# Sixty-eight sums of GpSimd move to VectorE and ScalarE, with 20 pause lists and 9 places of modulation chunks

## What is computed

```python
# first block
merged = sigmoid(gate_a) * y_a + sigmoid(gate_b) * y_b
x = x + merged @ w_out
h = rms_norm(x, ln2)
x = x + (silu(u_gate) * u_val) @ w_down          # u = causal_dwconv(h @ w_up)
# second block, for each of two layers
mod = silu(c) @ w_mod + b_mod                    # shift, scale, gate
h = rmsnorm(x, norm_gain) * (1 + scale) + shift
dots = einsum('bqhd,bsd->bqhs', q_idx, k_idx)    # indexer: 16 heads of 64
I = einsum('bqh,bqhs->bqs', w_idx, relu(dots))
sel = top_k(where(causal, I, -inf), 64)
logits = q_a @ k_a * scale + bias[rel]           # only where selected
att = softmax(logits) @ v_a
x1, x2 = halves(q_b or k_b)                      # rotary
rotated = [x1 * cos - x2 * sin, x1 * sin + x2 * cos]
ret = retention(q_b, k_b, v_b)                   # two chunks of 128
x = x + gate * (concat(att * silu(g_a), groupnorm(ret) * silu(g_b)) @ w_out)
```

## Time and profile before

| | us |
|---|---|
| median of 3 runs | 1931.37 (1929.94 to 1937.82) |
| the profiled execution, its own time | 1930.03 |
| its span on the core | 1928.2 |
| PE busy | 1834.6 (95%) |
| DVE busy | 1688.6 (88%) |
| ACT busy | 1230.3 (64%) |
| POOL busy | 213.0 (11%) |
| DMA engines, share of the span | 81.3% |
| granted TensorE clock, mean share | 0.979 |

### The profile page before, as it was taken

How to read it: one execution, slowest core, us unless ns; L and a number is a source line. 1 busy time by engine, 2 the same in 40 slices (tenths; PEclk the granted TensorE clock), 3 DMA queues, 4 the chain that set the end, 5 groups by cost and what they waited for, 6 DMA issues and landing times.

```text
span 1928.2 us, 33543 instructions
## 1 busy us (share of the span) xinstructions
PE 1834.6 (95%) x13102; PEld 1715.3 (89%) x13102; DVE 1688.6 (88%) x2199; ACT 1230.3 (64%) x1907; POOL 213.0 (11%) x140
## 2 busy tenths in 40 slices
PE   6999999999999999999999999899999999998998
PEld 5888899999997899889998997889889888987897
DVE  7897997988798799999999897898898889898896
ACT  6667654744664675656766667756668775657773
POOL 0000031031010001122000000042110003132000
PEclk9998999999999999999999999999999999999999
DMA  8887876968898897788999997877888878786985
GB/s 291 266 273 242 281 240 219 311 198 289 298 356 320 282 313 237 258 289 295 308 321 348 329 331 242 285 248 253 266 278 308 276 231 296 233 277 222 325 297 183
DMA packets 258523, 535.81 MB, mean 278 GB/s; under 512 B 23609, under 2 KB 28734, under 8 KB 257342
## 3 DMA queue, kind: packets, MB, share of 16 engines
q1 hardware_dynamic: 257933, 531.44, 81.3%
q10 hardware_dynamic: 432, 2.23, 0.3%
HBM read 531.50 MB, written 2.10 MB: 277 GB/s over the span
## 4 chain that ended last, share of the span: by engine, by line
PE 46%; DVE 10%; issue 4%; ACT 4%; DMA 1%; POOL 1%; SPq 0%; ACTq 0%; DVEq 0%
PE ps L151 46%; DVE ring_r L1900 3%; ACT w L1456 1%; DVE AR_r L1900 1%; DMA ring<-in_w_in 1%; POOL AR L2498 1%; DVE macc L1900 1%; ACT stg L1462 1%; DVE stg L1897 1%; DVE stg L1892 0%; ACT AR L1456 0%; DVE stg L1900 0%; ACT AR L1462 0%; DVE AR L1892 0%; DVE AR L2369 0%
## 5 line engine op out<-in xcount | busy, mean ns | idle before, releaser
L1900 DVE SCALAR_TENSOR_TENSOR ring_r<-ring,w 128x1024 fp32r<-128x1024 f32 x495 | 616.2, 1265 | 94.4 <-ACT w L1456 93.8
L1456 ACT ACTIVATE w<-ring 128x1024 fp32r<-128x1024 f32 x495 | 510.9, 1055 | 173.0 <-PE ps L151 84.6
L151 PE MATMUL ps<-hh_r,w 128*128 128x256 f32 (+1 forms) x3500 | 505.3, 287 | 7.1 <-ACT w L1456 5.6
L151 PEld LDWEIGHTS ps<-hh_r,w 128*128 128x128 f32 (+1 forms) x3500 | 453.1, 191 | 14.7 <-issue 7.0
L151 PE MATMUL ps<-hlo,ring_r 128*128 128x256 f32 x3108 | 435.9, 283 | 1.5 <-DVE ring_r L1900 1.5
L151 PEld LDWEIGHTS ps<-hlo,ring_r 128*128 128x128 f32 x3108 | 399.8, 190 | 1.7 <-DVE ring_r L1900 1.7
L1900 DVE SCALAR_TENSOR_TENSOR AR_r<-AR,w 128x1024 fp32r<-128x1024 f32 (+1 forms) x150 | 187.3, 1260 | 30.6 <-ACT w L1456 30.6
L151 PE MATMUL ps<-AR 128*128 128x64 f32 (+5 forms) x1316 | 181.8, 296 | 18.5 <-DVE AR L1896 6.2
L151 PEld LDWEIGHTS ps<-AR 128*128 128x128 f32 (+1 forms) x1316 | 165.2, 196 | 28.1 <-issue 9.9
L1456 ACT ACTIVATE w<-AR 128x1024 fp32r<-128x1024 f32 (+1 forms) x150 | 154.4, 1045 | 52.4 <-PE ps L151 31.2
L1900 DVE SCALAR_TENSOR_TENSOR macc<-ring,sm,macc 128x1024 f32<-128x1024 f32 x131 | 177.1, 1352 | 0.1
(11 more groups left out here) (221 smaller groups left out, 2269.4 us busy)
## 6 DMA issues: line engine op xcount, KB each, us to landing
ring<-in_w_in SPq DMA_DIRECT2D x313, 512.0 KB, 5.0
ring<-in_w_mod SPq DMA_DIRECT2D x142, 512.0 KB, 5.4
ring<-in_w_up SPq DMA_DIRECT2D x126, 512.0 KB, 5.3
ring<-in_w_down SPq DMA_DIRECT2D x66, 512.0 KB, 5.7
AR<-in_w_in SPq DMA_DIRECT2D x64, 512.0 KB, 5.5
ring<-in_w_out SPq DMA_DIRECT2D x64, 512.0 KB, 5.8
AR<-in_w_up SPq DMA_DIRECT2D x50, 512.0 KB, 5.5
AR<-in_w_mod SPq DMA_DIRECT2D x37, 512.0 KB, 5.6
```

Source lines behind the costliest of these rows:

```text
L151: return e.matmul(o, l, x, start=start, stop=stop, skip_group_check=True)
L1456: return e.activation(o, i, ACT.Copy, scale=scale)
L1900: return e.scalar_tensor_tensor(o, a, s, b, op0, op1)
```

## The change

The 68 sums of the four kinds leave POOL. Those of `merge`, `sparse` and `rot` (40) become `tensor_tensor` instructions on DVE in the same segment. In the indexer, segments 1 to 7, ACT takes the relu from the banks (4 activations a segment, 56 in all, on the same two pieces of each bank), and DVE multiplies by the weight and adds to the running sum in one `scalar_tensor_tensor` that reads the staging buffer and the sum, both in SBUF (4 a segment, in place of 4 `tensor_scalar`). The banks now go back when ACT is through, the staging buffers when DVE is.

In the tables, 20 pause lists are new or changed, for `bias`, `convk` (k, 2), `convq` (q, 3), `gdn` (2), `indexer` (1), three `modend`, four `retain`, two `sparse` and six `xpose`; and `MODS` gains nine entries. Most segments that move do so by one to four chunks; segments 13 to 21 of `bias` stand three chunks later and 22 to 37 seven.

```diff
-    ('bias',): (2, 2, 4, 1, 2, 4, 6, 0, 4, 1, 2, 4, 1, 2, 4, 1, 2, 4, 1, 2, 4, 1, 2, 4, 1, 2, 4, 1, 2, 4, 1, 2, 4, 1, 2, 4, 1),
+    ('bias',): (2, 2, 4, 1, 2, 4, 6, 0, 4, 1, 2, 4, 4, 2, 4, 1, 2, 4, 1, 2, 4, 5, 2, 4, 1, 2, 4, 1, 2, 4, 1, 2, 4, 1, 2, 4, 1),
...
-    ('retain', 1, 3): (4, 5, 2, 3, 4, 1, 1), ('setup',): (2, 2, 0, 1, 1), ('sparse', 0, 1): (4, 1, 1, 4, 3, 1),
...
+    ('sparse', 0, 1): (2, 3, 1, 4, 3, 1), ('sparse', 0, 3): (5, 1, 0, 5, 3, 1), ('xpose', 1, 0): (3, 1, 1),
...
@@ USES
-                *[f"+a +b +s +z -s@idx_pool.g0{i} -z@idx_pool.g1{i} -a@idx_dve.a{i} -b@idx_dve.b{i}"
+                *[f"+a +b +s +z -s@idx_dve.b{i} -z@idx_dve.b{i} -a@idx_act.a{i} -b@idx_act.b{i}"
...
@@ scalar_program
+        def indexer(J, seg):
+            L, = J.at
+            if 1 <= seg < 8:
+                hold(e, J, "s", "z")
+                x0, x1 = pair(st(J, "s")[:, 0:256]), pair(st(J, "z"))
+                e.wait_ge(*idx_pe.after(f"p{seg}", L))
+                for hf, bk in ((0, pb(J, "a")), (1, pb(J, "b"))):
+                    fn(x0[:, hf, :], bk[:, 0:128], ACT.Relu)
+                    fn(x1[:, hf, :], bk[:, 128:384], ACT.Relu).then_inc(*idx_act.step(f"{'ab'[hf]}{seg}", L))
...
-                e.wait_ge(*merge_pool.after("sum", blk, hf))
+                e.wait_ge(*merge_dve.after("sum", blk, hf))
@@ vector_program, merge
+                k = 4 * blk + 2 * hf
+                e.wait_ge(*merge_dve.after("gate", blk, hf))
+                e.wait_ge(*yb_dve.after(f"y{hf}", blk))
+                tt(s_, s_, flat2(GBT[:, k:k + 2, :]), ADD).then_inc(*merge_dve.step("sum", blk, hf))
@@ vector_program, indexer
+                        e.wait_ge(*idx_act.after(f"{'ab'[hf]}{seg}", L))
+                        e.wait_ge(*idx_dve.after(f"{'ab'[hf]}{seg - 1}", L))
+                        stt(a0[:, hf, :], x0[:, hf, :], wi[:, 0, hd:hd + 1], a0[:, hf, :], MUL, ADD)
+                        stt(a1[:, hf, :], x1[:, hf, :], wi[:, 1, hd:hd + 1], a1[:, hf, :], MUL, ADD).then_inc(*idx_dve.step(f"{'ab'[hf]}{seg}", L))
@@ vector_program, sparse
+                e.wait_ge(*idx_dve.after("sel1", L))
+                e.wait_ge(*bias_act.after("e11"))
+                if hp > 0:
+                    e.wait_ge(*sp_pe.after("pv", L, hp - 1))
+                tt(L0, B0[:, h0:h0 + 2, :], mid(MN0, 2), ADD).then_inc(*sp_dve.step("l0", L, hp))
+                tt(L1, B1[:, h0:h0 + 2, :], mid(MN1, 2), ADD).then_inc(*sp_dve.step("l1", L, hp))
                 e.wait_ge(*sp_pe.after("qk", L, hp))
                 e.wait_ge(*qn_dve.after("inv", L, hp))
-                e.wait_ge(*sp_pool.after("l1", L, hp))
+                e.wait_ge(*sp_dve.after("l1", L, hp))
@@ vector_program, rot
+                e.wait_ge(*rot_dve.after("m", *J.at))
+                tt(d, d, zv, ADD).then_inc(*rot_dve.step("sum", *J.at))
@@ pool_program: merge, indexer, sparse and rot are gone
```

More of the change, by code:

```diff
@@ L219 @@
                "+f -f@sp_act.out"],
-    "rot": ["+z", "-z@rot_pool.sum"],
+    "rot": ["+z", "-z@rot_dve.sum"],
     "retain": ["+s +z +a +b -a@ret_dve.s0 -b@ret_dve.s1", "+c -c@ret_act.out", "", "", "",
@@ L390, in program @@
     gb_act, yb_dve = signal("gb_act"), signal("yb_dve")
-    merge_act, merge_dve, merge_pool = (signal(f"merge_{n}") for n in ("act", "dve", "pool"))
+    merge_act, merge_dve = (signal(f"merge_{n}") for n in ("act", "dve"))
     resid_dve, half_dve, down_dve = signal("resid_dve"), signal("half_dve"), signal("down_dve")
@@ L397, in program @@
     ki_pe = signal("ki_pe")
[L398 removed]
+    idx_pe, idx_act, idx_dve = (signal(f"idx_{n}") for n in ("pe", "act", "dve"))
     kn_pe, kn_act, kn_dve, kn_pool = (signal(f"kn_{n}") for n in ("pe", "act", "dve", "pool"))
     qn_pe, qn_act, qn_dve = (signal(f"qn_{n}") for n in ("pe", "act", "dve"))
[L401 to L402 removed]
+    sp_pe, sp_act, sp_dve = (signal(f"sp_{n}") for n in ("pe", "act", "dve"))
+    rot_act, rot_dve = (signal(f"rot_{n}") for n in ("act", "dve"))
     ret_pe, ret_act, ret_dve = (signal(f"ret_{n}") for n in ("pe", "act", "dve"))
@@ L1403, in retain @@
                 hold(e, J, "a", "b")
-                e.wait_ge(*rot_pool.after("sum", L, "q", hp))
-                e.wait_ge(*rot_pool.after("sum", L, "k", hp))
+                e.wait_ge(*rot_dve.after("sum", L, "q", hp))
+                e.wait_ge(*rot_dve.after("sum", L, "k", hp))
                 for h in range(2):
@@ L1882, in scalar_program @@
                  "bias": bias, "ki": ki, "qi": qi, "vb": vb, "kn": kn, "qn": qn,
-                 "sparse": sparse, "rot": rot, "retain": retain, "glu": glu}
+                 "indexer": indexer, "sparse": sparse, "rot": rot, "retain": retain, "glu": glu}
         for what, *a in steps:
@@ L2338, in indexer @@
             if seg < 8:
-                e.wait_ge(*idx_pe.after(f"p{seg}", L))
                 if seg == 0:
+                    e.wait_ge(*idx_pe.after(f"p{seg}", L))
                     given_back(e, f"W{L}")
@@ L2344, in indexer @@
                 else:
-                    hold(e, J, "s", "z")
                     x0, x1 = pair(st(J, "s")[:, 0:256]), pair(st(J, "z"))
@@ L2517, in gdn @@
                 tt(G.AL, G.AT, mid(lev[:, l + 1, :], 4), MUL).then_inc(*gdn_pool.step(f"al{l + 1}", bt))
-        def merge(J, seg):
-            blk, hf = J.at
-            if seg == 1:
-                s_, k = st(J, "s"), 4 * blk + 2 * hf
-                e.wait_ge(*merge_dve.after("gate", blk, hf))
-                e.wait_ge(*yb_dve.after(f"y{hf}", blk))
-                tt(s_, s_, flat2(GBT[:, k:k + 2, :]), ADD).then_inc(*merge_pool.step("sum", blk, hf))
         def bias_in(J, seg):
@@ L2540, in bias @@
                    rep(PKC[:, 32 * kb + 8 * jh:32 * kb + 8 * jh + 8], 128), ADD).then_inc(*bias_pool.step(f"rel{i}"))
-        def indexer(J, seg):
-            L, = J.at
-            if 1 <= seg <= 7:
-                a0, a1 = carve(W2, 2, 128), carve(W2 + 256, 2, 256)
-                e.wait_ge(*idx_dve.after(f"b{seg}", L))
-                if seg > 1:
-                    e.wait_ge(*idx_pool.after(f"g1{seg - 1}", L))
-                tt(a0, a0, pair(st(J, "s")[:, 0:256]), ADD).then_inc(*idx_pool.step(f"g0{seg}", L))
-                tt(a1, a1, pair(st(J, "z")), ADD).then_inc(*idx_pool.step(f"g1{seg}", L))
         def kn(J, seg):
@@ L2557, in kn @@
                 tt(z, s_, s_, MUL).then_inc(*kn_pool.step("sq", *J.at))
-        def sparse(J, seg):
-            L, hp = J.at
-            L0, L1, mcol, rcol, PT0, PT1 = softmax_of(hp, 0, W2)
-            h0 = 2 * hp
-            if seg == 0:
-                e.wait_ge(*idx_dve.after("sel1", L))
-                e.wait_ge(*bias_act.after("e11"))
-                if hp > 0:
-                    e.wait_ge(*sp_pe.after("pv", L, hp - 1))
-                tt(L0, B0[:, h0:h0 + 2, :], mid(MN0, 2), ADD).then_inc(*sp_pool.step("l0", L, hp))
-                tt(L1, B1[:, h0:h0 + 2, :], mid(MN1, 2), ADD).then_inc(*sp_pool.step("l1", L, hp))
-        def rot(J, seg):
-            L, name, hp = J.at
-            if seg == 1:
-                d = (QB if name == "q" else KB)[:, 2 * hp:2 * hp + 2, :]
-                e.wait_ge(*rot_dve.after("m", *J.at))
-                tt(d, d, pair(st(J, "z")), ADD).then_inc(*rot_pool.step("sum", *J.at))
-        parts = {"gdn": gdn, "merge": merge,
-                 "biasin": bias_in, "bias": bias, "indexer": indexer, "kn": kn, "sparse": sparse, "rot": rot}
+        parts = {"gdn": gdn, "biasin": bias_in, "bias": bias, "kn": kn}
         for what, *a in steps:
```

29 lines of the change are left out of this document (17 added, 12 removed).

## The result

The changed kernel took 1903.14 us in the median of four executions (1897.39 to 1906.73), the kernel before, beside it, 1932.02. The forecast was a gain of 17 us, 1914 us in a range of 1901 to 1931. By the ratio the changed kernel takes 1899.9 us on the scale of 1931.37, just under that range. The direction was right, the size was not.

The account below looks back on a forecast made before the run. PE, busy 95% of the span, was taken as the bound, so only its waits and half clock could be won. Terms of -1.7, -6.4, -2.5, -5.3 and -1.5 sum to -17.4 us, giving 1914 us, range 1901 to 1931.

Parts of the forecast that it names:

- Relief of DVE: Over the whole span, sums leaving POOL speed up DVE's slowed remainders and modulation chunks: -24.5 us on DVE.
- Step 2: Rotary, sparse attention, retention: DVE's net saving counts in full on PE, -6.4 us, ends +18 and -22.9.
- step 1: Indexer: PE no longer waits for DVE to hand back the banks, since ACT does it: -1.7 us.
- Step 5: Merge: ACT and the rounded copies no longer wait for POOL's eight sums: -1.5 us, ends 0 and -5.
- step 4: Clock: three long PE waits become short enough to keep full clock: -5.3 us, ends 0 and -8.8.
- the waits move on: Rival: PE waits for the next late item and DVE's saved time turns idle: 1925 us, chance 0.24.
- More comes back: Rival: moved pauses remove waits at their places and DVE's relief nears its full 41.0 us: 1900 us, chance 0.15.
- Step 3: Softmax of sparse (0, 1): row maxima move ahead of the rotary products, removing one PE wait: -2.5 us.
- Step 6: The other moved pauses and modulation chunks: taken as 0, ends +5 and -8 us.
- The slower rivals: DVE becomes the bound, 1945 us, chance 0.06; ACT becomes the bound in the indexer, 1926 us, chance 0.03.
- The signs: Expected in the changed profile: softmax waits under 8 us, DVE busy 0 to 10 less, ACT 15 to 22 more.

Follow-up runs that it names:

- e1: The changed kernel with the old PAUSE and MODS tables, so only the 68 sums moved against the kernel before: ratio 0.9978 (0.996 to 0.9996).
- e2: The kernel before with only the new tables, all 68 sums still on POOL: ratio to before 0.9887 (0.9864 to 0.991).
- e13: The changed kernel measured again, with no further edit, against the kernel before: ratio 0.9846 (0.9825 to 0.9868).
- e4: The kernel before with only the indexer's 28 sums moved off POOL: ratio to before 1.0 (0.9978 to 1.0021).
- e17: The changed kernel with five more modulation chunks moved behind late items on DVE's queue: ratio to the kernel before 0.9857 (0.9834 to 0.9881).
- e8: The kernel before with one pause list added, retain (1, 2), segments 3 to 6 two chunks later: ratio to before 0.9971 (0.9952 to 0.9991).
- e3: The kernel before with only the eight sums of merge moved to DVE: ratio to before 0.9989 (0.9973 to 1.0006).
- e5: The kernel before with only the part of the new tables that acts up to 660 us: ratio to before 0.9943 (0.9922 to 0.9965).

## Why the prediction was wrong, step by step

- **Relief of DVE: right in size.** It said -24.5 us on DVE for 25.3 added. In e1, which has the same places as before, DVE is busy for 1685.3 us against 1688.6 with the added sums in; so 29 us or so came back (the means of the 128x1024 groups give 28.9).
- **Step 2 (-6.4) and what goes with the sums.** Steps 1, 2, 5 and one clock drop of step 4 come to 11.4 us for the sums, and e1 measured 4.3 (0.8 to 7.7; 8.5 by the medians). On top of the new tables they may be worth more: e2 against e13 is 7.9 us (6.1 to either side). "What DVE saves counts in full" was the mis-sized part, and within it "the indexer's part is handed on while DVE does not run dry" failed: DVE waits for ACT 4.8 us longer in the two indexers of e4, it runs dry again ahead of the softmax, as e17's rows show, and the indexer alone gave 0.0, the 1.7 us of step 1 among it. Of the rivals, *the waits move on* was right on this, and was weighed against the whole, not against this term. *More comes back* had the number (1900 us), but for half a reason: the pauses did remove waits at their own places, at 21.9 us and not 8, while DVE's relief was 29 us and not near 41.0.
- **Step 3 (-2.5): the move worked, and the sums took it back.** PE's wait for `sparse` (0, 1) is 2.8 us before and 2.9 after. With the sums alone it is 5.0, with the tables alone 1.8 (PE in e1, then in e2):

```profile
1354.64 0.45 PE L1178 MATMUL ps<-cst,AR 128*128 128x128 f32 x1 [5.03 <-ACT AR L1456]
```

```profile
1348.19 0.30 PE L1183 MATMUL ps<-cst,AR 128*128 128x128 f32 x1 [1.79 <-ACT AR L1461]
```

  So the tables are worth 1.0 us at this wait without the sums and 2.1 with them, and the sums on DVE cost 1.1 to 2.2 there, which the prediction had not booked against it. The maxima stand ahead of the rotary now, but DVE's next item of this softmax, a reciprocal of 0.17 us, still stands behind the six rotary instructions and a remainder, and ACT, which scales by it, waits 5.48 us. DVE and ACT in e13:

```profile
1343.90 0.69 DVE L1907 TENSOR_TENSOR AR<-AR 128x512 f32<-128x512 f32 x1
1344.51 1.22 DVE L1915 SCALAR_TENSOR_TENSOR ring_r<-ring,w 128x1024 fp32r<-128x1024 f32 x1
1345.65 0.17 DVE L2105 RECIPROCAL sm<-sm 128x4 f32<-128x4 f32 x1
```

```profile
1345.85 1.49 ACT L1461 ACTIVATE AR<-AR,sm 128x128 f32<-128x128 f32 x4 [5.48 <-DVE sm L2105]
```

  A wait that is the last of a chain goes only if all its links come earlier.
- **Step 4 (-5.3): right in kind, the size is open.** The granted clock in the first stretch is 1.00 against 0.95 in the earlier trace rows, 0.98 in the second as before, and PE is busy for 7.0 us less in the two. Over the whole span it is only 1.7 us less (1832.9 against 1834.6), and in e13, the same kernel, 8.8. Behind `retain` (1, 2) it is 1.00 (against 0.50):

```profile
1805.00:1808.50 3.50, 2.98 (x26) 2.81 (x25) 3.50 (x5) 2.04 (x3) 0.00 (x0) 1.00 1.04 412
```

  The half clock went with the wait. Without the table entry, in e1, this wait is still 2.9 us, and with the entry alone, in e8, it is gone.
- **Step 5 (-1.5):** e3 has 2.1, not told from nothing. The 7.6 us won behind the merges are mostly of the tables: e5 gives 11.0 with POOL's sums in place.
- **Step 6 (0, ends +5 and -8): the step that failed.** It put the other moved pauses and modulation chunks at nothing. With step 3 and its share of the clock, the forecast had some 6 us for the tables; they are worth 21.9 alone and 25.6 on top of the sums (e1 against e13, 5.4 to either side). "No row prices them, and each can win or lose at most a wait of the size of those in the earlier trace rows" has the price in it: with 29 entries and a dozen waits of 1 to 4.4 us, the bound had to be the sum of the waits that an entry touches, not one of them. The forecast came as near as it did by luck in part: about 7 us too much for the sums stand against some 16 too little for the tables. In the trace of before PE waited at items that the new tables move, or that have a moved DVE item ahead, for 4.0 us (`modend` (1, 0)), 4.4 (`retain` (1, 2)) and smaller ones; the four groups of the earlier trace rows alone are 25.7 us. That an entry touches each of these is not shown, and in e2 the softmax still waits for 10.5 us, so this bound is loose.
- **The slower rivals** did not come: no remainder stayed long without POOL, and ACT had its 56 relus at 278 and 393 ns with no wait of PE in the indexers.
- **The signs:** the softmax transposes still wait 9.0 us (under 8 was forecast), ACT is busy for 13.5 us more (15 to 22), and DVE does wait for relus, 3.0 us at the smaller form. DVE's busy time (-8.6) and the end of the waits for POOL came as forecast.
